# Channel vectors and the turned block matrix laid out by the host, and the order of the first loads

## What is computed

```
first block, for l in 0, 1:
    x = x + token_mixer(rmsnorm(x, norm1_g[l]), ...)      # pooling, gated block mixing (sgu), short convolution
    x = x + swiglu(rmsnorm(x, norm2_g[0]), ...)           # l = 0: dense, width 3584
    x = x + moe_ffn(rmsnorm(x, norm2_g[1]), ...)          # l = 1: 8 experts, two per token
x = rmsnorm(x, final_g)
second block, for l in 0, 1:
    x = x + 0.5 * swiglu(rms_norm(x, ffn1_norm[l]), ...)  # width 2816
    x = x + mixer(rms_norm(x, mix_norm[l]))               # latent attention and a 31-tap convolution
    x = x + 0.5 * swiglu(rms_norm(x, ffn2_norm[l]), ...)
    x = rms_norm(x, post_norm[l])

sgu:  mixed = einsum("hij,bnjhc->bnihc", w_s * mask, vn) + b_s     # w_s: 4 heads of 128 x 128 per layer
```

## Time and profile before

| | us |
|---|---|
| median of 3 executions | 2518.7 (2518.01 to 2520.75) |
| the profiled execution | 2518.03 |
| its span, first to last instruction | 2515.9 |
| PE busy | 2394.9 |
| DVE busy | 1904.4 |
| ACT busy | 1443.2 |
| POOL busy | 27.1 |

### The profile page before, as it was taken

How to read it: one execution, slowest core, us unless ns; L and a number is a source line. 1 busy time by engine, 2 the same in 40 slices (tenths; PEclk the granted TensorE clock), 3 DMA queues, 4 the chain that set the end, 5 groups by cost and what they waited for, 6 DMA issues and landing times.

```text
span 2515.9 us, 33477 instructions
## 1 busy us (share of the span) xinstructions
PE 2394.9 (95%) x12192; PEld 2019.7 (80%) x12192; DVE 1904.4 (76%) x1947; ACT 1443.2 (57%) x1489; POOL 27.1 (1%) x49
## 2 busy tenths in 40 slices
PE   5999999999999999999999989997999999988998
PEld 4888888788888888888888778875888788866886
DVE  5676667788888888888888876678666766687765
ACT  3554444677777776777777654446544544455543
POOL 3000000000000000000000000000000000000000
PEclk9999999899999999999999989998999999998999
DMA  5555544699999999999999945532355555432552
GB/s 196 174 185 194 184 160 163 245 374 339 372 342 371 343 371 342 372 342 371 342 365 348 358 155 184 186 128 85 134 184 185 174 184 189 152 108 88 185 193 85
DMA packets 83869, 594.37 MB, mean 236 GB/s; under 512 B 9920, under 2 KB 10242, under 8 KB 12626
## 3 DMA queue, kind: packets, MB, share of 16 engines
q1 hardware_dynamic: 81216, 587.76, 64.5%
q0 software_dynamic: 2000, 4.50, 0.6%
q10 hardware_dynamic: 582, 1.16, 0.1%
HBM read 592.33 MB, written 1.05 MB: 236 GB/s over the span
## 4 chain that ended last, share of the span: by engine, by line
PE 86%; DVE 9%; ACT 2%; DMA 1%; issue 1%; ACTq 0%; DVEq 0%
PE banks L1006 16%; PE banks L1059 9%; PE banks L1061 9%; PE banks L1065 9%; PE banks L1008 8%; PE banks L1084 8%; PE banks L1086 8%; PE banks L1085 8%; DVE acc L2022 4%; PE banks L1035 2%; PE banks L1179 1%; DVE lo L1592 1%; DVE xhl L1679 1%; PE banks L1100 1%; DMA stage_rows<-in_sgu_b 1%; PE banks L969 1%
## 5 line engine op out<-in xcount | busy, mean ns | idle before, releaser
L1592 DVE TENSOR_TENSOR lo<-raw,hi 128x2048 fp32r<-128x2048 f32 x550 | 1258.5, 2290 | 224.9 <-ACT hi L556 221.5
L556 ACT CAST hi<-raw 128x2048 fp32r<-128x2048 f32 x550 | 1051.8, 1913 | 258.6 <-PE banks L1065 119.0
L1006 PE MATMUL banks<-xhl,hi 128*128 128x512 f32 x1776 | 629.5, 398 | 1.2 <-DVE gsum L1633 1.2
L1008 PE MATMUL banks<-xhl,lo 128*128 128x256 f32 x1776 | 498.3, 281 | 0.0
L1006 PEld LDWEIGHTS banks<-xhl,hi 128*128 128x128 f32 x1776 | 333.6, 188 | 84.2 <-DVE lo L1592 1.6
L1084 PE MATMUL banks<-hi,xhl 128*128 128x512 f32 x896 | 354.4, 396 | 0.8 <-issue 0.8
L1086 PE MATMUL banks<-hi,xhl 128*128 128x512 f32 x896 | 350.3, 391 | 0.0
L1085 PE MATMUL banks<-lo,xhl 128*128 128x512 f32 x896 | 349.6, 390 | 0.0
L1059 PE MATMUL banks<-hi,hh 128*128 128x512 f32 x872 | 343.0, 393 | 1.8 <-DVE hl L1604 1.8
L1061 PE MATMUL banks<-lo,hh 128*128 128x512 f32 x872 | 340.7, 391 | 0.0
L1008 PEld LDWEIGHTS banks<-xhl,lo 128*128 128x128 f32 x1776 | 335.3, 189 | 1.9
(11 more groups left out here) (367 smaller groups left out, 2457.4 us busy)
## 6 DMA issues: line engine op xcount, KB each, us to landing
raw<-in_moe_w_gate SPq DMA_DIRECT2D x112, 1024.0 KB, 4.9
raw<-in_moe_w_up SPq DMA_DIRECT2D x112, 1024.0 KB, 4.9
raw<-in_moe_w_down SPq DMA_DIRECT2D x112, 1024.0 KB, 4.9
raw<-in_ffn_w_gate SPq DMA_DIRECT2D x58, 1024.0 KB, 4.9
raw<-in_ffn_w_up SPq DMA_DIRECT2D x58, 1024.0 KB, 4.9
raw<-in_ffn_w_down SPq DMA_DIRECT2D x58, 1024.0 KB, 4.8
raw<-in_mix_pieces SPq DMA_DIRECT2D x46, 1024.0 KB, 4.9
raw<-in_mix_pieces SPq DMA_DIRECT2D x2, 768.0 KB, 4.1
```

Of the source, the lines that this page charges most:

```text
L556: nc.scalar.copy(hi[:, hslot(S, c), 0:n], raw[:, c % RING, 0:n]).then_inc(S.hi_done, 1)
L1006: pe.matmul(bank[b + s][:, :], hi[:, hr, a:a + P], xhl[:, k, :], start=(k == 0), stop=False, skip_group_check=True)
L1008: mm = pe.matmul(bank[b + s][:, 0:T], lo[:, r, a:a + P], xhl[:, k, 0:T], start=False, stop=(k == KD - 1), skip_group_check=True)
L1592: v.tensor_tensor(lo[:, c % RING, 0:n], raw[:, c % RING, 0:n], hi[:, hslot(S, c), 0:n].bitcast(F32), ALU.subtract).then_inc(S.lo_done, 1)
```

## The change

The host writes all channel vectors into one array `chan` of 128 x 4 x 128 floats, in the layout that the kernel's tile of that name has, and the block matrix already transposed as `sgu_turned`. ACT loads `chan` in one load straight behind x, and POOL loads `sgu_turned` into `wsT` as the last of its first loads. The turns of both on PE, the copies on DVE, and the scratch tiles are gone. The order of the start changes too. SP issues piece 0 and waits for both halves of x before piece 1. POOL makes the token count first and waits for x before its small loads. ACT loads the table for square roots before it rounds piece 0, and rounds piece 1 behind the high parts of x and ahead of the squares. DVE makes its constants ahead of the rests of pieces 0 and 1. The products of gains, `fold`, and the zeroed corner of `wsT` become `later_constants`, which DVE does in the first mixing stage ahead of the norm of the outer groups; ACT waits for `gains_ready` before the second norm, and PE for the constants before the block mixing.

```diff
@@ SP, first mixing stage
+                        if l == 0 and m == 1:
+                            for t in range(TT):
+                                sp.wait_ge(x_loaded[t], 16)
                         sp_load(sp, main, st["B"] + m, 0, A["mix1_pieces"][l, m], PIECE)
@@ ACT, act_norm
-            nc.scalar.preload_act_table(ACT.Sqrt)
+            if M:
+                nc.scalar.preload_act_table(ACT.Sqrt)
             for k in range(KD):
...
                                      scale=col(("gain", M), k)).then_inc(xh_done, 1)
+            if not M:
+                act_hi(act, main, st["B"] + 1, 0)
@@ ACT, start
-            for tile, at, n, ap in staged[::2]:
-                act.dma_start(stage_rows[at:at + n, tile, :], ap).then_inc(ev("rows_in"), 16)
-            act_ahead(act, stages[0])
-            act.wait_ge(ev("gains_ready"), 1)
+            act.dma_start(chan[:], A["chan"]).then_inc(ev("chan_in"), 16)
+            nc.scalar.preload_act_table(ACT.Sqrt)
+            act_hi(act, main, stages[0]["B"], 0)
+            act.wait_ge(ev("chan_in"), 16)
             for st in real:
                 k = st["kind"]
+                if st is real[1]:
+                    act.wait_ge(ev("gains_ready"), 1)
@@ PE, pe_mix1, ahead of the block mixing
             pe.wait_ge(ev("vn_out"), 2 * (l + 1))
+            if l == 0:
+                pe.wait_ge(ev("const_pool"), N_POOL)
+                pe.wait_ge(ev("const_vec"), N_VEC)
@@ PE, start
-        def pe_constants(pe):
...
-            for tile, n in enumerate(used):
-                pe.transpose(bank[0][:, tile * P:tile * P + n], stage_rows[0:n, tile, :],
-                             ident[0:n, 0:n]).then_inc(ev("chan_turned"), 1)
-            pe.wait_ge(ev("ws_in"), 16)
...
-            pe_constants(pe)
@@ POOL
-            for tile, at, rows, ap in staged[1::2]:
-                pool.dma_start(stage_rows[at:at + rows, tile, :], ap).then_inc(ev("odd_rows_in"), 16)
-            pool.dma_start(stage_ws[:], A["sgu_w"].rearrange("l h i j -> i l h j")).then_inc(ev("ws_in"), 16)
+            g.iota(invc[:], pattern=[[0, 2], [1, T]], base=1, channel_multiplier=0,
+                   allow_small_or_imprecise_dtypes=True).then_inc(ev("counted"), 1)
             link(g.memset(ones[:], 1.0))
...
+            for t in range(TT):
+                pool.wait_ge(x_loaded[t], 16)
             for dst, src in small:
                 pool.dma_start(dst, src).then_inc(ev("small_in"), 16)
...
+            pool.dma_start(wsT[:], A["sgu_turned"]).then_inc(ev("ws_in"), 16)
@@ DVE, mix1
+                if l == 0:
+                    later_constants()
                 group_norm(((0, 0, DP), (2, DP + DS, D)), slice(0, 3, 2), 6 * l + 4, 1)
@@ DVE, constants
-                dve.wait_ge(ev("const_pool"), N_POOL)
+                dve.wait_ge(ev("counted"), 1)
...
-                note(v.reciprocal(invc[:], invc[:]))
-                dve.wait_ge(ev("chan_turned"), len(used))
-                for tile, n in enumerate(used):
-                    note(v.tensor_copy(chan[:, tile, 0:n], bank[0][:, tile * P:tile * P + n]))
-                settle()
+                link(v.reciprocal(invc[:], invc[:]))
+
+            def later_constants():
                 for st in real:
                     if post_before(st):
                         a, b = col(("gain", st["M"]), 0, KD), col(("post", post_before(st)["layer"]), 0, KD)
                         link(v.tensor_tensor(a, a, b, ALU.mult))
                 note(v.tensor_tensor(fold[:, :], ident[0:2 * NE, 0:NE], ident[0:2 * NE, NE:2 * NE], ALU.add))
                 mark(ev("gains_ready"))
-                for l in range(2):
-                    dve.wait_ge(ev("ws_turned"), l + 1)
-                    note(v.tensor_copy(wsT[:, l, :, :], bank[(3, 1)[l]][:, :].rearrange("p (h i) -> p h i", h=SH)))
-                settle()
-
+                dve.wait_ge(ev("ws_in"), 16)
                 v.memset(wsT[64:P, :, :, 0:64].rearrange("p l h i -> p (l h) i"), 0.0).then_inc(ev("const_vec"), 1)
                 dve.wait_ge(ev("const_vec"), N_VEC)
 
-            for s in range(2):
-                lo_piece(main, s, 0)
             constants()
+            lo_piece(main, 0, 0)
             turned_rest_x(0, range(KD))
+            lo_piece(main, 1, 0)
+            dve.wait_ge(ev("const_pool"), N_POOL)
@@ host
+    a["chan"] = np.zeros((P, 4, P), np.float32)
+    for tile, at, _, source, layer, n in chan_rows():
+        vectors = a[source] if layer is None else a[source][layer]
+        a["chan"][:, tile, at:at + n] = vectors.reshape(n, P).T
+    a["sgu_turned"] = a["sgu_w"].transpose(3, 0, 1, 2)
```

More of the change, by code:

```diff
@@ L111, in plan, with chan_rows, put @@
     return stages
+def chan_rows():
+    gain = dict(mix1="norm1_g", ffn1="norm2_g", moe="norm2_g", ffn2a="ffn1_norm_2", mix2="mix_norm_2",
+                ffn2b="ffn2_norm_2")
+    rows, used = [], [0, 0, 0, 0]
+    def put(tile, name, source, layer, n):
+        rows.append((tile, used[tile], name, source, layer, n))
+        used[tile] += n
+    for st in plan():
+        if st["kind"] != "post":
+            put(3, ("gain", st["M"]), gain[st["kind"]], 1 if st["kind"] == "moe" else st["layer"], KD)
+    put(3, ("post", 0), "final_g", None, KD)
+    put(3, ("post", 1), "post_norm_2", 0, KD)
+    for l in range(2):
+        put(0, ("group", l), "group_g", l, KD)
+        put(0, ("cw", l), "conv_w", l, CW * 2)
+        put(0, ("cb", l), "conv_b_2", l, 4)
+        put(0, ("clg", l), "conv_ln_g_2", l, 4)
+        put(0, ("clb", l), "conv_ln_b_2", l, 4)
+        put(0, ("ql", l), "q_latent_norm_2", l, QL // P)
+        put(0, ("kvl", l), "kv_latent_norm_2", l, KVL // P)
+        put(0, ("sb", l), "sgu_b", l, SH)
+        put(1 + l, ("cw2", l), "conv_w_2", l, CK * 4)
+    return rows
 def build(nc, A, rope, hide, out):
@@ L213, in __call__ @@
                 return t
-        s0 = Scratch()
-        stage_rows = s0("stage_rows", [P, 4, P])
-        stage_ws = s0("stage_ws", [P, 2, SH, P])
         s1 = Scratch()
@@ L331, in ev, with gain_of @@
             return E[name]
[L334 to L349, removed]
+        where = {name: (tile, at) for tile, at, name, source, layer, n in chan_rows()}
+        def gain_of(p):
+            return A["final_g"] if p["layer"] == 0 else A["post_norm_2"][p["layer"] - 1]
         whole_at = [st["B"] + m for st in stages if st["kind"] == "mix2" for m in MIX2_WHOLE]
@@ L1450, in pe_router @@
               .then_inc(ev("count_out"), 1)
-        def pe_constants(pe):
-            pe.wait_ge(ev("rows_in"), 16 * len(staged[::2]))
-            pe.wait_ge(ev("odd_rows_in"), 16 * len(staged[1::2]))
-            for tile, n in enumerate(used):
-                pe.transpose(bank[0][:, tile * P:tile * P + n], stage_rows[0:n, tile, :],
-                             ident[0:n, 0:n]).then_inc(ev("chan_turned"), 1)
-            pe.wait_ge(ev("ws_in"), 16)
[L1460 to L1465, removed]
         @block.tensor
@@ L1526, in _ @@
             g.iota(slots[:], pattern=[[1, P]], base=0, channel_multiplier=0,
-                   allow_small_or_imprecise_dtypes=True).then_inc(ev("const_pool"), 1)
-            g.iota(invc[:], pattern=[[0, 2], [1, T]], base=1, channel_multiplier=0,
                    allow_small_or_imprecise_dtypes=True).then_inc(ev("const_pool"), 1)
@@ L2269 @@
 N_SMALL = 8
-N_POOL = 4
+N_POOL = 3
 N_VEC = 2
@@ L2319, in laid_out @@
             for l, m in enumerate(mix2)]
+    a["chan"] = np.zeros((P, 4, P), np.float32)
[3 more added lines that the diff above has]
+    a["sgu_turned"] = a["sgu_w"].transpose(3, 0, 1, 2)
     a["mix1_pieces"] = np.stack([np.stack(p) for p in mix1])
     a["mix2_pieces"] = np.stack([np.concatenate([p.reshape(-1) for p in ps]) for ps in mix2])
-    for name in ("w_in", "w_out", "w_in_2", "w_uq_2", "w_ukv_2", "w_out_2"):
+    for name in ("w_in", "w_out", "w_in_2", "w_uq_2", "w_ukv_2", "w_out_2", "norm1_g", "ffn1_norm_2", "mix_norm_2",
+                 "ffn2_norm_2", "group_g", "conv_w", "conv_b_2", "conv_ln_g_2", "conv_ln_b_2", "q_latent_norm_2",
+                 "kv_latent_norm_2", "sgu_b", "sgu_w", "conv_w_2"):
         del a[name]
```

## The result

The changed kernel takes 2495.89 us (median; 2495.49 to 2498.41), the kernel before 2518.36 (2517.08 to 2520.75) beside it. The ratio is 0.9913, with a 95% interval of 0.9898 to 0.9928: **faster by 22.5 us**, where 2496 was forecast. The profiled execution took 2495.84 us with a span of 2494.1, against 2518.03 and 2515.9.

The account below looks back on a forecast made before the run. PE, busy 95% of the span, was taken as the bound, its start held by the late vector loads. 2518.0 - 22.2 = 2495.8, taken as 2496 us (chance 0.72); range 2491 to 2503.

Parts of the forecast that it names:

- Step (1): Start loads: x lands at 8.9 us, at latest 11.5; the channel vectors at 9.5, at latest 12.2.
- Steps (2) and (3): Start: x turned 8.9 to 12.6, low parts done 14.9, first weight matmul at 15.2: 22.2 us gone.
- Step (5): First piece: piece 1 lands 14.4, scale ready 19.7, cover 4.0 us; long end (10.0) scale 24.2, costing 0.5 us.
- Step (6): Later pieces: piece 3 there at 22.6 if all POOL's loads went ahead, slot free at 23.9; in time, by little.
- Step (7): POOL's loads behind x: pooling weights there by 29, used at 35.6; block matrix lands near 30, wanted near 47.
- Step (8): First mixing stage: moved gain products, fold and zeroed corner take about 1.2 us, hidden in DVE's 5.20 us of idle time.
- Rival (a): PE's first piece: full clock granted at once, 5.9 us at the low level shrink by 2.6, giving 2493.2; chance 0.13.
- Every later stage earlier by the same 22 us: Sign to look for after the start: the end of every later stage moves earlier by the same 22 us.
- wrong if the gain at 100 us is not the gain at the end: Test over the later stages: the forecast is wrong if the gain at 100 us differs from that at the end.
- the assumption of the first paragraph: Whole kernel: time saved where PE stands still reaches the end if nothing later has its own start time.
- The range's 2 us for the later stages: Allowance at both ends of the range for later stages of PE at the low clock differing between executions: 2 us.

## Why the prediction was right, step by step

**Step (1), right.** x was there at 1.26 + 7.3 = 8.6 (8.9 forecast), the vectors at 9.2 (9.5). Its late end for the vectors, 12.2, was too low: without SP's wait they came at 14.15.

**Steps (2) and (3), right.** Turns from 8.72, last low part at 14.81 (14.9), PE at 14.85 against 15.2: 0.2 us because the issue took 0.04 and not 0.25, and 0.1 in the low parts. x came 0.3 sooner, which gave nothing, as the step says. 22.55 us instead of 22.2. Without DVE's order 12.2 us of it are gone, and the layout alone brings 10.5.

**Step (5), right.** Piece 1 landed at 8.7 + 5.1 = 13.8 (14.4), the scale was ready at 19.0 (19.7), PE's first piece ended at 22.24 and the turn stood straight behind it, cover 3.2 us. Its long end was real: 10.4 us in the run without POOL's wait, with the scale at 24.3 (24.2). Beside a first piece that ends at 22.2, and not at 23.7, that is 2.1 us instead of 0.5.

**Step (6), right in the verdict, with no margin left.** Piece 3 landed at 9.5 + 12.7 = 22.2 against 22.6, but PE's first piece ended at 22.24 and not at 23.7. A difference of 0.04 us is no margin; with PE sooner by 2, the piece was the bound.

**Step (7), right, one load mis-sized.** The block matrix came at 34.1, not near 30; it took 17.1 us from issue, with 12.3 as the row taken. DVE was only there at 46.4.

**Step (8), right.** DVE's wait for PE fell from 5.20 to 3.94, by 1.26 us, with 1.2 forecast for the moved work.

**Rival (a), given 0.13, came half true in the profiled execution, and that was luck.** PE rested 2.5 us behind its turns, began at the high level for 1.5 us, fell to the low one for 3.2, and rose again. Its first piece took 7.4 us instead of 8.5: 1.15 us of the rival's 2.6. The forecast's argument against it, that the turns themselves had not lifted the clock, failed here: the clock did come up while nothing but the rest lay between the turns and the weight matmuls. But it isn't shown to be the change's work. In the run with ACT padded by half PE rested 2.4 us as well, its matmuls stood 0.21 us apart until 20.7, and the piece took 8.5 us as before. With the layout alone it rested 10.6 us, and the piece took 7.3. Over the nine kernels in which PE waits for all low parts and not for the scale, the piece took 7.2 to 8.5 us, in no order of the rests. The Trainium skill (TensorE: Matmul & The Clock Gate, Part 1) says that sustained work lifts the clock and an idle stretch drops it; the trace agrees that both happen, and here the drop shows only 1.5 us after the restart.

**What was in no step.** "Every later stage earlier by the same 22 us" failed, and with it the own test "wrong if the gain at 100 us is not the gain at the end": it was 23.7 and then 21.8. The step that failed is the assumption of the first paragraph, that what is saved where PE stands still reaches the end as long as nothing has a start time of its own. The later stages' code was not changed, but ACT's place in its program was, and the stall that came with it lies where the 2.5 us were lost; how much of them it cost the runs only bound; the rest moves with the clock in the stage changes, about 1 us at a time. So the time came within 0.1 us of the sum partly by compensation, which is luck: +0.35 (start) and +1.15 (clock) were met by -1.9 later on, and what lies around the span was 1.7 us instead of 2.1, for which the forecast had no term. The range's 2 us for the later stages was the right size, and was needed.

## What to carry to other kernels

Ask of a late start what each input would be late by if the others came at once: here the loads' layout, their order and one engine's own queue each held it, and half of the gain hung on a reordering on DVE that none of the loads' rows points to. Behind the start, count a wait of PE at half again to twice its length if the granted clock is at half behind it (4.3 us cost 6.1, 2.2 us cost 4), which made one wait per stage, split by chunk, worth more than half of this whole change. And when small loads are put off for one transfer, look which transfer they meet instead.

## What the hardware did that was not expected

- ACT stood still for 4.8 to 5.3 us behind a conditional block that isn't taken when its program was 14 or 7 instructions shorter than before, and not at all with 14 instructions of filler.
- PE behind a rest of 2.5 us: high level for 1.5 us, low for 3.2, high again, all under full load; in another program with a rest of 2.4 us at the same place: low for 5.9 us, then high. There the granted column read 1.00 all the time, as in the kernel before, and only the matmuls' distance told. Behind a rest of 4.3 us: low for 6 us at once.
- POOL's thirteen loads (1.5 MB) queued 5.4 us earlier doubled the landing of a 1 MB piece, 5.1 to 10.4 us. A 256 KB load in 2 KB rows needed 12.4 us beside the pieces and 7.5 with them held back.
